# A third buffer for the split expert rows, and 28 expert tiles done in two parts by tokens

## The reference, cut to what matters

```
a   = gelu(u_tab[e] . x)                 # one number per pick
out = sum over picks of gate * a * v_tab[e]
```

## Time and profile before

| | |
|---|---|
| Median of three runs | 3297.57 us (3292.72 to 3304.71) |
| The profiled execution | 3285.14 us, its span in the trace 3283.3 us |
| PE busy in the span | 2876.8 us (88%) |
| DVE busy | 2371.1 us (72%) |
| POOL busy | 1287.0 us (39%) |
| Stages by the trace | K2 925 to 1961, D2 to 2046, gates to 2237, tail to 2271, down to 3283 |

### The profile page before, as it was taken

How to read it: one execution, slowest core, us unless ns; L and a number is a source line. 1 busy time by engine, 2 the same in 40 slices (tenths; PEclk the granted TensorE clock), 3 DMA queues, 4 the chain that set the end, 5 groups by cost and what they waited for, 6 DMA issues and landing times. The chain is left out here.

```text
span 3283.3 us, 42515 instructions
## 1 busy us (share of the span) xinstructions
PE 2876.8 (88%) x15144; PEld 2529.0 (77%) x15144; DVE 2371.1 (72%) x5095; ACT 815.6 (25%) x1242; POOL 1287.0 (39%) x1088
## 2 busy tenths in 40 slices
PE   6999999799999999897999988999887676758888
PEld 4777777669999999897989968998765455547676
DVE  5676555446678888886788878994655667669995
ACT  4323323223212212211122112442211111112223
POOL 0000000001135565564555540002777777775540
PEclk9999999899999999998999998999988788879999
DMA  4112110223378998998888872779977788889992
GB/s 162 40 53 66 41 40 27 104 104 136 105 279 307 336 355 315 342 356 308 324 328 317 315 283 68 230 235 326 355 262 257 265 296 287 298 286 404 407 382 103
DMA packets 294113, 780.21 MB, mean 238 GB/s; under 512 B 31880, under 2 KB 97932, under 8 KB 291776
## 3 DMA queue, kind: packets, MB, share of 16 engines
q0 software_dynamic: 124832, 424.38, 35.9%
q1 hardware_dynamic: 102288, 316.01, 26.2%
q10 hardware_dynamic: 66832, 37.78, 3.9%
HBM read 679.89 MB, written 98.18 MB: 237 GB/s over the span
## 5 line engine op out<-in xcount | busy, mean ns | idle before, releaser
L1261 PE MATMUL u_p<-hn_hi,u_hi 128*128 128x384 f32 x2048 | 713.6, 348 | 87.5 <-DVE u_lo L1250 79.5
L1262 PE MATMUL u_p<-hn_lo,u_hi 128*128 128x384 f32 x2048 | 705.0, 344 | 0.0
L1263 PE MATMUL u_p<-hn_hi,u_lo 128*128 128x384 f32 x2048 | 704.0, 344 | 0.0
L2080 POOL DMA_INDIRECT y_ring<-in_peer_v,row_idx x320 | 393.9, 1231 | 491.5 <-POOLq L1880 324.2
L2130 PE MATMUL y_p<-v_hi,w_hi 128*128 128x512 f32 x1024 | 352.5, 428 | 217.2 <-DVE w_lo L2213 217.2
L1261 PEld LDWEIGHTS u_p<-hn_hi,u_hi 128*128 128x128 f32 x2048 | 396.1, 193 | 94.4 <-DVE u_lo L1250 84.9
L1697 POOL DMA_INDIRECT s_ring<-in_peer_u,row_idx x264 | 321.9, 1219 | 286.8 <-DVE s_dots L1827 172.4
L2130 PEld LDWEIGHTS y_p<-v_hi,w_hi 128*128 128x128 f32 x1024 | 207.7, 208 | 281.1 <-DVE w_lo L2213 232.4
L2225 DVE SCALAR_TENSOR_TENSOR y_late<-y_ring,row_weight,y_late 128x1024 f32<-128x1024 f32 x256 | 329.5, 1287 | 116.5 <-DMA y_ring<-in_peer_v,row_idx 98.1
L1262 PEld LDWEIGHTS u_p<-hn_lo,u_hi 128*128 128x128 f32 x2048 | 396.1, 193 | 0.0
L1263 PEld LDWEIGHTS u_p<-hn_hi,u_lo 128*128 128x128 f32 x2048 | 395.7, 193 | 0.0
(11 more groups left out here) (393 smaller groups left out, 4595.5 us busy)
## 6 DMA issues: line engine op xcount, KB each, us to landing
u_raw<-in_peer_ut SPq DMA_DIRECT2D x128, 512.0 KB, 6.8
act_scratch<-act_tile SPq DMA_DIRECT2D x128, 384.0 KB, 4.5
late<-in_peer_v SPq DMA_DIRECT2D x32, 1024.0 KB, 7.4
down_raw<-in_peer_v SPq DMA_DIRECT2D x32, 1024.0 KB, 5.9
wp_raw<-in_w_heads SPq DMA_DIRECT2D x64, 256.0 KB, 3.3
late<-in_w_query SPq DMA_DIRECT2D x16, 1024.0 KB, 7.1
gate_scratch<-gbuf ACTq DMA_DIRECT2D x4, 4096.0 KB, 21.0
gate_scratch<-late ACTq DMA_DIRECT2D x4, 4096.0 KB, 20.8
```

What stands on the lines that cost most here:

```text
L1261: mm(b, uh[:, s, k, :], hn_hi[:, k, t], start=(k == 0), stop=False)
L1262: mm(b, uh[:, s, k, :], hn_lo[:, k, t], start=False, stop=False)
L1263: last = mm(b, ul[:, s, k, :], hn_hi[:, k, t], start=False, stop=(k == ND - 1))
L2080: nc.gpsimd.indirect_dma_start(out=ring[:, n % RING, :], out_offset=None, in_=A["peer_v"], in_offset=bass.IndirectOffsetOnAxis(ap=idx[:, c ...
```

## The change

`u_hi` and `u_lo` get a third buffer, and in ACT's list `u_hi` of tile e + 2 moves ahead of tile e's gelu. The job list grows from 128 to 156: 28 expert tiles are split into a LATER job (tokens 512 to 767, 24 products of 256 columns) and an EARLY job (tokens 0 to 511, 24 products of 512). The LATER jobs are spread over K2, two in each of its first 14 sections of seven jobs; sections 15 and 16 have five full tiles. The EARLY jobs are the 24 of the gates, one behind each of steps 1, 4 and 7 of eight (counted from 0), and the 4 of the tail. In the gates ACT's `u_hi` and DVE's `u_lo` of tile e + 2 both stand behind the step that tile e follows. So all activations of tokens 512 to 767 are stored when the gates begin, and POOL fetches 144 of the 256 picks there; the other 112 stay in the down stage, two for every three rows. Of the V-row adds 168 instead of 192 are done in K2, over its last 6 sections, and 88 instead of 64 in the down stage. Activations of the two token groups go to two DRAM tensors. The diff, cut (of the new helpers only the new lines):

```diff
-E_K1, E_D1, E_K2, E_D2 = 10, 4, 88, 6
-E_GATES = 2 * NSUB
+NLATE = 28
+E_K1, E_D1, E_K2, E_D2 = 10, 4, 80 + NLATE, 6
+E_GATES = 3 * NSUB
 G0 = E_K1 + E_D1 + E_K2 + E_D2
-K2_ADDS = 192
+K2_ADDS = 168
+PICKS = 144
+FULL, LATER, EARLY = range(3)
+NJOB = NK + NLATE
+KINDS = ([FULL] * (E_K1 + E_D1) + [FULL, LATER, FULL, FULL, LATER, FULL, FULL] * (NLATE // 2) + [FULL] * (10 + E_D2)
+         + [EARLY] * NLATE)
...
-        a_dram = nc.dram_tensor("act_scratch", (NK, P, DENSE), F32, kind="Internal").ap()
+        a_dram = nc.dram_tensor("act_scratch", (NK, P, VD), F32, kind="Internal").ap()
+        a_late = nc.dram_tensor("late_act_scratch", (NK, P, NG2), F32, kind="Internal").ap()
...
+            picked = wt[:, NG:NG + NG2]
...
-    uh, ul = (sb(own, "u_" + x, [P, 2, ND, P], F32R) for x in ("hi", "lo"))
+    uh, ul = (sb(own, "u_" + x, [P, 3, ND, P], F32R) for x in ("hi", "lo"))
...
+    def expert(e):
+        if not isinstance(e, int):
+            return e - NLATE
+        if e >= G0:
+            return e - NLATE
+        return sum(KINDS[x] == FULL for x in range(e)) if KINDS[e] == FULL else NK - NLATE + sum(
+            KINDS[x] == LATER for x in range(e))
+    def u_load(sp, e, r, first=False):
         if not first:
             sp.wait_ge(ulo_done, e - 1)
+        sp.dma_start(u_raw[:, r % 2], A["peer_ut"][expert(e)]).then_inc(u_in[r % 2], 16)
+    def a_store(sp, e, r, kind):
         sp.wait_ge(gelu_done, 2 * e + 2)
+        if kind != LATER:
+            sp.dma_start(a_dram[expert(e)], av[:, r % 2, 0:VD]).then_inc(a_out[r % 2], 16)
+        if kind != EARLY:
+            sp.dma_start(a_late[expert(e)], av[:, r % 2, VD:DENSE]).then_inc(l_out[r % 2], 16)
+    def u_high(act, e, r, half):
+        act.wait_ge(u_in[r % 2], 16 * half + 16)
+        if not (isinstance(e, int) and e < 3):
+            act.wait_ge(up_done, 2 * e - 4)
+        nc.scalar.activation(uh[:, r % 3], u_raw[:, r % 2], ACT.Copy).then_inc(uhi_done, 1)
+    def u_low(eng, ops, e, r):
         eng.wait_ge(uhi_done, e + 1)
+        ops.tensor_tensor(ul[:, r % 3], u_raw[:, r % 2], uh[:, r % 3].bitcast(F32), ALU.subtract).then_inc(ulo_done, 1)
+    def u_products(pe, b, r, t, count):
         mm = nc.tensor.matmul
+        for k in range(ND):
+            mm(b, uh[:, r % 3, k, :], hn_hi[:, k, t], start=(k == 0), stop=False)
+            mm(b, uh[:, r % 3, k, :], hn_lo[:, k, t], start=False, stop=False)
+            last = mm(b, ul[:, r % 3, k, :], hn_hi[:, k, t], start=False, stop=(k == ND - 1))
+        last.then_inc(up_done, count)
+    def u_unit(pe, e, g):
         if g == 0:
             pe.wait_ge(ulo_done, e + 1)
+        if e:
             pe.wait_ge(gelu_done, 2 * e + g - 1)
+        u_products(pe, pu[g][:, 0:CH], e, slice(g * CH, (g + 1) * CH), 1)
+    def part(kind):
+        return slice(0, VD) if kind == EARLY else slice(VD, DENSE)
+    def u_part(pe, e, r, kind, behind_full):
+        t = part(kind)
+        pe.wait_ge(ulo_done, e + 1)
+        pe.wait_ge(gelu_done, 2 * e - 1 + r % 2 if behind_full else 2 * e - 2)
+        u_products(pe, pu[r % 2][:, 0:t.stop - t.start], r, t, 2)
+    def u_gelu(act, e, g):
         act.wait_ge(up_done, 2 * e + g + 1)
+        if g == 0 and e >= 2:
+            main = sum(KINDS[x] == FULL for x in range(e % 2, e, 2))
+            act.wait_ge(a_out[e % 2], 16 * main)
+            act.wait_ge(l_out[e % 2], 16 * (e // 2))
+        nc.scalar.activation(av[:, e % 2, g * CH:(g + 1) * CH], pu[g][:, 0:CH], ACT.Gelu).then_inc(gelu_done, 1)
+    def part_gelu(act, e, r, kind, stores):
+        t = part(kind)
+        act.wait_ge(up_done, 2 * e + 2)
+        act.wait_ge((a_out if kind == EARLY else l_out)[r % 2], 16 * stores)
+        nc.scalar.activation(av[:, r % 2, t], pu[r % 2][:, 0:t.stop - t.start], ACT.Gelu).then_inc(gelu_done, 2)
     def tile_in(sp, e):
+        if e + 3 < NJOB:
+            u_load(sp, e + 3, e + 3)
+        a_store(sp, e, e, KINDS[e])
     def tile_products(pe, e):
+        if KINDS[e] == FULL:
+            for g in range(2):
+                u_unit(pe, e, g)
+        else:
+            u_part(pe, e, e, KINDS[e], KINDS[e - 1] == FULL)
+    def early_stores(e):
+        return sum(KINDS[x] != LATER for x in range(e % 2, e, 2))
     def tile_out(act, e):
+        if e + 2 < NJOB:
+            u_high(act, e + 2, e + 2, (e + 2) // 2)
+        if KINDS[e] == FULL:
+            for g in range(2):
+                u_gelu(act, e, g)
+        else:
+            part_gelu(act, e, e, KINDS[e], early_stores(e) if KINDS[e] == EARLY else e // 2)
...
-            SD = 9
-            FIRST_U = [E0 + 11 * (s // 2) + 6 * (s % 2) for s in range(NSEC + 1)]
+            SD = 10
+            FIRST_U = [E0 + 7 * min(s, NLATE // 2) + 5 * max(s - NLATE // 2, 0) for s in range(NSEC + 1)]
...
-                        if s + 1 < NSEC and i == 3:
+                        if s + 1 < NSEC and i == n - 3:
                             chunk(s + 1)
-                        if s + 1 < NSEC and i == 4:
+                        if s + 1 < NSEC and i == n - 2:
...
-                        e = FIRST_U[s] + i + 1
-                        if e <= FIRST_U[s + 1]:
-                            u_low(dve, nc.vector, e, e % 2)
+                        a, z = (FIRST_U[s] + (FIRST_U[s + 1] - FIRST_U[s]) * x // 6 + 1 for x in (i, i + 1))
+                        for e in range(a, z):
+                            u_low(dve, nc.vector, e, e)
...
+        BEHIND = (1, 4, 7)
...
+        @block.gpsimd
+        def _(pool):
+            acts = a_late.rearrange("e p (t o) -> (e p t) o", o=1)
+            for p in range(2):
+                pool.wait_ge(l_out[p], 16 * (G0 // 2))
+            for c in range(PICKS):
+                nc.gpsimd.indirect_dma_start(
+                    out=picked[:, c:c + 1], out_offset=None, in_=acts,
+                    in_offset=bass.IndirectOffsetOnAxis(ap=idx[:, NU + NG2 + c:NU + NG2 + c + 1], axis=0)
+                ).then_inc(act_in[c // SUB], 16)
...
+                for x in range(6):
+                    e = G0 + 6 * j + x
+                    u_load(sp, e + 3, G0 + x + 3)
+                    a_store(sp, e, x, EARLY)
...
-                        if n % 2:
-                            u_unit(pe, G0 + 4 * j + 2 * s + n // 4, n // 4, n // 2 % 2)
-            for e in range(R0, NK):
+                        if n in BEHIND:
+                            x = 3 * s + BEHIND.index(n)
+                            u_part(pe, G0 + 6 * j + x, G0 + x, EARLY, False)
...
-                        if n % 2:
-                            p, half = n // 4, G0 // 2 + 2 * j + s
-                            e = G0 + 4 * j + 2 * s + p
-                            u_gelu(act, e, p, n // 2 % 2, half)
-                            if n // 2 % 2:
-                                u_high(act, e + 2, p, half + 1)
+                        if n in BEHIND:
+                            x = 3 * s + BEHIND.index(n)
+                            e = G0 + 6 * j + x
+                            u_high(act, e + 2, G0 + x + 2, G0 // 2 + 3 * j + (x + 2) // 2)
+                            part_gelu(act, e, x, EARLY, STORED[x % 2] + 3 * j + x // 2)
                     act.wait_ge(bank_out, (2 * NSTEP) * (2 * j + s + 1) + 4)
...
-                        if n % 4 == 3:
-                            u_low(dve, nc.vector, G0 + 4 * j + 2 * s + n // 4 + 1, (n // 4 + 1) % 2)
+                        if n in BEHIND:
+                            x = 3 * s + BEHIND.index(n) + 2
+                            u_low(dve, nc.vector, G0 + 6 * j + x, G0 + x)
...
-    FROM = [1, 18, 58]
+    FROM = [1, 15, 58]
...
-            for p in range(2):
-                pool.wait_ge(a_out[p], 16 * (NK // 2))
-            for n in range(RING, KEPT + RING):
-                for c in range(2):
-                    pick(2 * (n - RING) + c)
+            c = PICKS
+            for n in range(RING, NADD):
                 row(n)
-            for n in range(KEPT + RING, NADD):
-                c = 2 * KEPT + n - KEPT - RING
-                if c < NG2:
+                while c < min(NG2, PICKS + (n - RING + 1) * 2 // 3):
                     pick(c)
-                row(n)
+                    c += 1
```

More of the change, by code:

```diff
@@ L1206, in mixer_stages, with up_phase @@
     return hn_hi, hn_lo
-def up_phase(nc, A, own, sb, ps, sem, ident, hn, x2_dram, hs_dram, g_dram, a_dram, ysb, yt, idx, wt, gate_tok, av, late, picks_dram,
-             first_query, old):
+def up_phase(nc, A, own, sb, ps, sem, ident, hn, x2_dram, hs_dram, g_dram, a_dram, a_late, ysb, yt, idx, wt, gate_tok, picked, av, late,
+             picks_dram, first_query, old):
     hn_hi, hn_lo = hn
@@ L1219, in up_phase @@
     e3s = sb(own, "e3s", [P, 3, NS])
-    eb = sb(own, "e_half", [P, 2, VD], F16)
-    gp = sb(own, "gate_parts", [P, 2, VD], F16)
     pu = [ps(own, f"u_p{g}") for g in range(2)]
-    u_in, a_out = ([sem(f"{x}{i}") for i in range(2)] for x in ("u_in", "a_out"))
```

(19 more changed lines are left out.)

83 lines of the change are left out of this document (25 added, 58 removed).

## The result

The changed kernel takes 3250.96 us (median of four runs, 3243.56 to 3253.34) against 3298.47 beside it: a ratio of 0.9852, 95% interval 0.9827 to 0.9876. It is faster by 47.5 us, clear of the spread of the runs though under 2%, where I forecast 119, and the time is 6 us above my range.

A forecast was written before the change was run, and what follows sets the result against it. No engine bounds the whole: PE in the gates, `u_lo` waits in K2, POOL's list then DMA and DVE in the down stage. 3285.1 - 139 (down) - 37 (K2) - 11 (tail) + 68 (gates) = 3166, plus 12.5: 3179 us; range 3105 to 3245.

The forecast's parts named there:

- K2, the third buffer: K2: ACT rounds a tile earlier, removing 13 PE waits for `u_lo` of 3.9 us and 13 slow restarts, -78 us.
- K2 gives nothing back: Rival in K2: loads come late behind LATER jobs, K2 at its upper end, 3222 us; chance 0.10.
- K2, the parts: K2: 80 full tiles of 8.43 us and 28 LATER parts of 2.85 replace 88 full tiles, +12 us.
- The gelu waits: K2: PE waits for gelu around LATER jobs, which use one bank, 21 times 0.7 us, +15 us.
- The 14 us that I took besides: K2: late loads hold up ACT's `u_hi` and the gelu behind it, 1 us per section, +14 us.
- Gates: Gates: DVE waits for `u_hi` of tile e + 2 and PE behind it, 24 times 2.83 us, +68 us.
- rival (1): Gates: DVE's wait for `u_hi` stays hidden and the 68 us do not come, 3111 us; chance 0.16.
- rival (5): Gates: PE's clock stays at its lower level through the tiles, +53 us, 3232 us; chance 0.04.
- Down: Down stage: POOL's list loses 144 picks and gains 24 rows, 873 us against 1012, -139 us.
- Picks in the gates: Gates: 144 picks take POOL 198 us, hidden beside a stage of 285 us, at no cost.
- Tail: Tail behind the gates: four EARLY jobs of 5.62 us replace four tiles of 8.43 us, -11 us.
- K2's upper end: K2: the top of the range -52 to +6 us around its forecast sum of -37 us.

The follow-up runs named there:

- gates_halves: Changed kernel with DVE's `u_lo` one tile later in the gates and PE's tiles there in two groups of 256 columns: 3180.0 us, ratio 0.9655.
- k2_weights_early: Changed kernel with ACT rounding the next head's query weights three tiles earlier in K2, not behind the section's last gelu: 3188.1 us, ratio 0.9683.

## Why the prediction was wrong, point by point

**K2, the third buffer: the step that failed.** I wrote that "ACT can round a tile one tile (8.4 us) earlier, which is more than DVE waits there; DVE arrives earlier and PE need not wait", and took away 13 waits. DVE did arrive earlier, and stood 8.24 us for the query weights, one list position further on. I asked what is late next in the down stage and not here, though the row was to be had: DVE's wait for `late_r` was 12.1 us in six in K2 before the change. In the sections without weights the step was right. With the weights early K2 and D2 lose 57 us against before, more than the 37 I forecast; as it was, they grew by 2.2 us, inside my -52 to +6 and close to the rival that "K2 gives nothing back", though by another cause than late loads.

**K2, the parts.** Sizes hold. A LATER tile of 24 x 256 columns runs from 1025.69 to 1028.5, 2.83 us (2.85). The gelu waits are 7.6 us where `u_lo` waits cover some, and 14.5 once those are gone (7.6 + 6.9), against 15. The 14 us that I took besides, for loads that hold up the gelu, did not show: ACT's waits for loads of U in K2 rose from 53.5 to 286.8 us, but those 14.5 us are all that PE waited for gelu there.

**Gates: the number right in part by luck, half of the cause missing.** +74 against +68, with DVE's 23 waits of 3.2 us at the place I named. But taking them away gave 31 us (267.5 to 236.4), and cutting PE's piece another 33 (to 203.4). I had compared the two lists by their sums (24.4 and 24.1 us) and not asked how far DVE can run ahead in a piece of 5.62 us. So rival (1), the waits hidden and the stage at its old length, could not have come about by hiding `u_hi` alone. That is the order in which the two edits were made; the other order was not run. I had put PE's clock at nothing. From the first step to the last, PE's busy time rose from 192 us at a granted clock of 0.97 (2034 to 2229 before) to 213 at 0.92 (2050 to 2320), and was 196 at 0.98 in gates_halves; how much of the +74 the clock makes is not shown, and rival (5), with all tiles at the lower level, did not come about.

**Down: mechanism right, size off by 25.** The four pieces are 17, 428, 354 and 98 us against 12, 423, 351 and 87. I had begun the end 12 us behind the last row; counted from that row on it is 98 us after and 99 before. I had also miscounted the rows before: the first stretch of the earlier trace rows holds 72 (its 200 instructions of POOL less 128 picks), not 64, and the last 120, not 128. So POOL's stretches ran 1% over their lists, not 3%, and the first part after ran 4% over. The rows without picks went at 246 / 119 = 2.07 us before (2938.1 to 3184.3), not 2.03; taking 2.03 was two errors that nearly cancel, and by the same rule 2.07 gives 2.13 where 2.12 was measured (353.9 / 167).

**Picks in the gates: right.** 151.5 us busy and 43.6 of issue are 195 against 198; the last starts at 2243, well inside the block. **Tail:** -10 against -11. **K1:** +6.2 by a load that I had not followed past the query weights in SP's list.

**The range.** 39 for K2, 25 for down, 6 each for K1 and the gates and 1 for the tail are the 78 us between 3166 and the 3244 that the profile has without the mixer's 8. I set the range by one rival at a time; here K2's upper end, the down stage and K1 came together, all on one side.

## What to carry to other kernels

When a buffer is added so that an engine may run ahead, read that engine's list onwards from the old wait and find the next thing it asks of another engine; the buffer is worth what lies between the two, and an edit that moves the second wait may be worth more than the buffer. Two in-order lists with equal sums still wait for each other when one has a piece that is longer than the buffers between them let the other run ahead. And add up the terms' ends for a range as well as the rivals, since small misses may lie on one side.

## What the runs showed of the hardware

The price of a wait on PE was not its length alone. After 4.53 us without work the next 15 products of 384 columns took 4.96 us from start to start (1033.34 to 1038.30), at a granted clock of 0.50, the lower of its two levels (1.2 GHz); a little later they go at 0.175 us each, 2.6 for 15. After 2.06 us without work (1025.69) the 24 of 256 columns took their 2.83 us, at 1.00. So removing the waits gave back more than the waits list shows: k2_weights_early took 47 us off PE's waits for `u_lo` in K2 and D2 (71.5 to 24.5), added 7 to those for gelu (7.6 to 14.5), and took 59 off K2 and D2.

A pick in the gates took 945 to 2000 ns, median 956, while DVE's 280 instructions did not lengthen. In the changed kernel's trace 27 of the 144 picks fell into DVE's waits, and took 946 to 957 ns; all 63 that took over 1.0 us had DVE at work beside them. The Trainium skill, page "SBUF — State Buffer", section "Who interferes with whom", says that the order of issue decides which of the two engines is blocked; the rows agree in that POOL was lengthened, by up to 1.05 us, and none of them shows the other case, DVE blocked by a pick.
